# All 32 cache pages of the samples issued from GpSimd's queue, in order, each as its buffer comes free

## The reference, cut to what matters

```python
k_p, v_p = shared_kv(hp, kv_norm, w_kv, pos_p)
k_s, v_s = shared_kv(hs, kv_norm, w_kv, pos_s)
n_seq = page_table.shape[0]                                   # 8 samples
k_past = cache_k[page_table].reshape(n_seq, -1, ATTN_N_HEADS, 2, ATTN_HEAD_DIM)
v_past = cache_v[page_table].reshape(n_seq, -1, ATTN_N_HEADS, ATTN_V_DIM)

def diff_attn_sample(q, k_past, v_past, k_new, v_new, lam):
    s_past = jnp.einsum('bqhjd,bkhjd->bhjqk', q, k_past).astype(jnp.float32) * scale
    s_new = jnp.einsum('bqhjd,bkhjd->bhjqk', q, k_new).astype(jnp.float32) * scale
    ...
    p = jax.nn.softmax(jnp.concatenate([s_past, s_new], axis=-1), axis=-1)
    att = (p[:, :, 0] - lam * p[:, :, 1]).astype(v_new.dtype)
    return (jnp.einsum('bhqk,bkhe->bqhe', att[..., :past], v_past) + jnp.einsum('bhqk,bkhe->bqhe', att[..., past:], v_new))
```

## Time and profile before

| | us |
|---|---|
| runs: median of 3 (lowest, highest) | 1665.21 (1665.15, 1666.52) |
| profiled execution, its own time | 1660.28 |
| its span, first to last instruction | 1658.4 |
| PE busy | 1570.6 (95%) |
| DVE, ACT, POOL busy | 944.6, 717.6, 16.5 |
| mean granted TensorE clock, share of 2.4 GHz | 0.953 |

### The profile page before, as it was taken

How to read it: one execution, slowest core, us unless ns; L and a number is a source line. 1 busy time by engine, 2 the same in 40 slices (tenths; PEclk the granted TensorE clock), 3 DMA queues, 4 the chain that set the end, 5 groups by cost and what they waited for, 6 DMA issues and landing times.

```text
span 1658.4 us, 29697 instructions
## 1 busy us (share of the span) xinstructions
PE 1570.6 (95%) x12252; PEld 1490.1 (90%) x12252; DVE 944.6 (57%) x1577; ACT 717.6 (43%) x1590; POOL 16.5 (1%) x20
## 2 busy tenths in 40 slices
PE   7999789997999999999999999998989999999997
PEld 6999556996899999999998988887878999999997
DVE  5667777799536742245346868852235752344435
ACT  5435445899425541243224436653245542134321
POOL 0000010000000000000000000000000000000000
PEclk8999999998899999999999999997579999999998
DMA  4222100564221322222222134431412322232221
GB/s 147 82 77 90 39 21 14 204 229 178 77 92 62 115 90 80 99 102 90 90 89 78 64 106 150 141 128 65 139 59 69 103 90 90 77 109 96 77 102 52
DMA packets 46088, 160.15 MB, mean 97 GB/s; under 512 B 5122, under 2 KB 7554, under 8 KB 45954
## 3 DMA queue, kind: packets, MB, share of 16 engines
q1 hardware_dynamic: 45954, 158.25, 27.9%
HBM read 142.07 MB, written 16.16 MB: 95 GB/s over the span
## 4 chain that ended last, share of the span: by engine, by line
PE 78%; DVE 11%; ACT 5%; DMA 4%; issue 2%; SPq 0%; DVEq 0%; ACTq 0%
PE GP L514 17%; PE GP L515 17%; PE GP L516 17%; PE WP L514 5%; PE WP L515 5%; PE WP L516 5%; PE WP L897 2%; DMA sssm<-hs 1%; PE GP L848 1%; DMA hs<-ssm_in 1%; DVE wL L1380 1%; PE GP L672 1%; PE WP L870 1%; ACT ht L1121 1%; PE GP L659 1%
## 5 line engine op out<-in xcount | busy, mean ns | idle before, releaser
L514 PE MATMUL GP<-hidH,wH 128*128 128x260 f32 x1408 | 414.5, 294 | 4.6 <-DVE hidL L1561 4.6
L514 PE MATMUL GP<-aH,wH 128*128 128x260 f32 x1376 | 395.9, 288 | 11.3 <-DVE aL L1406 5.8
L515 PE MATMUL GP<-hidL,wH 128*128 128x260 f32 x1408 | 401.9, 285 | 0.0
L516 PE MATMUL GP<-hidH,wL 128*128 128x260 f32 x1408 | 401.1, 285 | 0.0
L515 PE MATMUL GP<-aL,wH 128*128 128x260 f32 x1376 | 392.1, 285 | 0.0
L516 PE MATMUL GP<-aH,wL 128*128 128x260 f32 x1376 | 391.7, 285 | 0.0
L1380 DVE TENSOR_TENSOR wL<-wraw,wH 128x1024 fp32r<-128x1024 f32 x216 | 260.8, 1222 | 100.9 <-ACT wH L1003 100.5
L1003 ACT ACTIVATE wH<-wraw 128x1024 fp32r<-128x1024 f32 x216 | 225.4, 1053 | 153.7 <-DMA wraw<-wblk 152.9
L514 PEld LDWEIGHTS GP<-hidH,wH 128*128 128x128 f32 x1408 | 269.5, 191 | 10.4 <-DVE hidL L1561 5.5
L514 PEld LDWEIGHTS GP<-aH,wH 128*128 128x128 f32 x1376 | 262.6, 191 | 14.4 <-issue 11.1
L515 PEld LDWEIGHTS GP<-hidL,wH 128*128 128x128 f32 x1408 | 269.9, 192 | 1.9 <-issue 1.5
(11 more groups left out here) (268 smaller groups left out, 2228.5 us busy)
## 6 DMA issues: line engine op xcount, KB each, us to landing
wraw<-wblk SPq DMA_DIRECT2D x216, 512.0 KB, 3.4
hs<-ssm_in SPq DMA_DIRECT2D x16, 512.0 KB, 3.6
sssm<-hs SPq DMA_DIRECT2D x16, 512.0 KB, 4.5
ktile<-kcache SPq DMA_DIRECT2D x16, 512.0 KB, 4.0
vtile<-vcache SPq DMA_DIRECT2D x16, 512.0 KB, 5.6
hT<-x_t SPq DMA_DIRECT2D x4, 520.0 KB, 6.5
kt_out<-kT SPq DMA_DIRECT2D x4, 520.0 KB, 6.6
vt_out<-vT SPq DMA_DIRECT2D x4, 520.0 KB, 5.1
```

The source lines that it names most:

```text
L514: pe.matmul(out, lh, rh, start=first, stop=False)
L515: pe.matmul(out, lh, rl, start=False, stop=False)
L516: return pe.matmul(out, ll, rh, start=False, stop=last)
```

## The change

SP's loop loses all page issues, with their `value_load`s and the waits on `ss_s` and `pv_mm`. It keeps weight loads and outputs. GpSimd gets the 32 issues behind its products: first the key pages, page n as soon as page n - 2 has been scored, then, when all 16 pages have been scored, the value pages, page n as soon as the `page_values` that read buffer n % 4 before has ended. The conditions on which a buffer counts as free are those of before. PE, DVE and ACT run the same instructions in the same order.

```diff
@@ -448,35 +448,11 @@
-        sp.wait_ge(pt_in, 16)
-
-        def page(n, cache, dst, i, s):
-            idx = sp.value_load(ptile[0:1, n:n + 1], min_val=0, max_val=cache.shape[0] - 1)
-            sp.dma_start(dst[:, i, :, :].rearrange("p h k -> p (h k)"),
-                         cache[bass.ds(idx, 1), :, :].rearrange("o p n -> p (o n)")).then_inc(s[i], 16)
-
         kvb = BLOCK0["kv"] + RING
         stream(kb, kvb)
-        sp.wait_ge(done, PLACE["kv", 0, 0])
-        for n in range(2):
-            page(n, kcache, ktile, n, kp_in)
         for t in range(37):
             if t % 2 and t < STEPS:
                 load(kvb + t // 2)
-            if t - 1 in SPREAD_AT:
-                for n in range(2 * SPREAD_AT[t - 1] + 2, 2 * SPREAD_AT[t - 1] + 4):
-                    if n < NB * PAGES:
-                        sp.wait_ge(ss_s, n - 1)
-                        page(n, kcache, ktile, n % 2, kp_in)
-            if t == 23:
-                sp.wait_ge(ss_s, NB * PAGES)
-                for n in range(4):
-                    page(n, vcache, vtile, n, vp_in)
-            if PAGES_AT.get(t - 1, NB) + 2 < NB:
-                b = PAGES_AT[t - 1]
-                sp.wait_ge(pv_mm, b + 1)
-                for n in (2 * b + 4, 2 * b + 5):
-                    page(n, vcache, vtile, n % 4, vp_in)
             if t % 8 == 0 and t >= 8:
@@ -506,6 +482,23 @@
+        def page(n, cache, dst, i, s):
+            idx = pool.value_load(ptile[0:1, n:n + 1], min_val=0, max_val=cache.shape[0] - 1)
+            pool.dma_start(dst[:, i, :, :].rearrange("p h k -> p (h k)"),
+                           cache[bass.ds(idx, 1), :, :].rearrange("o p n -> p (o n)")).then_inc(s[i], 16)
+
+        pool.wait_ge(pt_in, 16)
+        pool.wait_ge(done, PLACE["kv", 0, 0])
+        for n in range(NB * PAGES):
+            if n >= 2:
+                pool.wait_ge(ss_s, n - 1)
+            page(n, kcache, ktile, n % 2, kp_in)
+        pool.wait_ge(ss_s, NB * PAGES)
+        for n in range(NB * PAGES):
+            if n >= 4:
+                pool.wait_ge(pv_mm, n // 2 - 1)
+            page(n, vcache, vtile, n % 4, vp_in)
```

## The result

The changed kernel takes 1653.39 us (median of 20 runs; the kernel before beside it 1666.46). The ratio is 0.9926, 95% interval 0.9908 to 0.9945, that is 12.3 us less, with bounds of 9.2 and 15.3. One of the 20 runs of the kernel before took 2533 us; without it their median is 1666.40. Two later comparisons gave 0.9944 (0.9926 to 0.9962) and 0.9942 (0.9919 to 0.9964), 9 to 10 us less. The forecast was 9.8 less and 1655.4. The profiled execution took 1651.82, its span 1650.1.

The account below looks back on a forecast made before the run. TensorE, 95% busy, was taken to lose time to value pages 4 and 5 standing in SP's queue behind a waiting load; -7.4 - 2.8 + 0.4 = -9.8 us, so 1665.2 to 1655.4 us, range 1651 to 1664.5.

Parts of the forecast that it names:

- The wait: TensorE's 7.4 us wait for a value page ahead of the value pass for sequence 2 goes away: -7.4 us.
- The pass of sequence 2: The value pass right behind the stall starts at full clock, taking a mean 4.2 us against 6.96: -2.8, bounds -3.5 and 0.
- What follows the pass: Work behind the value pass for sequence 2 runs at a somewhat lower clock: +0.4 us, bounds 0 and 0.8.
- Value pages 0 to 3: First four value pages, issued some 6 us earlier, first used at 1110.84: 0 us, hidden before and after.
- SP's loads at 0: Weight loads left in SP's queue are still issued when TensorE ends a half tile: 0 us gained.
- Key pages: Key pages issued from POOL stay covered ahead of VectorE's products: 0 us, upper bound +3.6.
- the price of an issue: For POOL's pages, buffer free to landed takes 5 to 6 us, bounds 4.7 and 9.7; a pair's second page some 1 us more.
- the limit: Sign against the price step: a landing time of over 8 us for a page issued by POOL would break it.
- rival 1: Without the stall's rest the clock falls around the value passes and takes back 9.6 us: no change, 1665.0 us; 7%.
- another queue saves only issue time: Rival: moving page issues to POOL wins only the 1.1 us step between two issues: no change, 1664.1 us; 7%.
- POOL did not hold VectorE: Rival judged here: POOL's 16 key page issues each hold VectorE 1.02 us, +6.5 in sum: slower, 1671.7 us; 10%.
- the better outcome: Rival: denser work holds the clock up behind sequence 2 and through sequence 3, 1.8 and 1.2 us more: 1652.4 us; 6%.

## Why the prediction was right, and where it was not

**The cause was right.** The stall was a place in SP's program order. Moving the pair ahead of the load on SP itself gives the gain, and putting the wait back on POOL takes it away.

**The wait, -7.4:** P1 to P2 fell from 18.04 to 10.62, by 7.42. This term carried most of the sum and came out as read.

**The pass of sequence 2, -2.8 (bounds -3.5 and 0):** it fell from 6.96 to 3.47, by 3.49, the bound. The clock was 1.00 throughout (stretch of the changed kernel):

```profile
1135.20:1138.70 3.50, 3.50 (x35) 3.48 (x33) 0.00 (x0) 1.97 (x4) 0.00 (x0) 1.00 0.42 150
```

The term was mis-sized by the choice of a mean over three passes. Two of them, 4.32 and 4.70, were slowed in part (granted clock 0.84 and 0.70), the third, 3.47, was not (1.00). Those two had begun in a stretch at 1.00 just as this pass was forecast to, so the rows did not say which of them it would follow. In the nine executions without the stall it took 3.47 to 3.74.

**What follows the pass, +0.4:** P2 to P3 without the pass was 11.81 and is 11.72, so nothing.

**Value pages 0 to 3, "0, hidden both times":** this step failed. The pages themselves are hidden, but the forecast asked only who waits for the pages, not what they are put ahead of. It had read that POOL would issue them some 6 us earlier, and it put SP's loads at 0, since they "stay gated by PE"; the load's issue is indeed gated, but the gate does not fix when it lands. The landing grew from 3.8 to 7.36 us and cost +1.84 (1.4 and 1.2 in the other two executions).

**Key pages and the price of an issue:** no loss, as forecast. Timeline of DVE (the reduction that frees the buffer of key page 4) and, in a second fence, the list of DMAs (KB each, median us from issue to landing), both of the changed kernel:

```profile
996.24 1.22 DVE L1735 TENSOR_REDUCE sT<-ktile 128x16 f32<-128x1024 f32 x1
```

```profile
wraw<-wblk SPq DMA_DIRECT2D x216, 512.0 KB, 3.4
...
ktile<-kcache POOLq DMA_DIRECT2D x16, 512.0 KB, 3.6
vtile<-vcache POOLq DMA_DIRECT2D x16, 512.0 KB, 4.3
```

From the end of the work that frees a buffer to the issue it took 1.8 us for key page 4 (end at 996.24 + 1.22 = 997.46, issue 999.24) and 1.2 us for value page 4 (1114.23 + 3.71 = 1117.94, issue 1119.15); the landings of the key pages took 3.6 us in the median, those of the value pages 4.3. That is 5.4 and 5.5, where 5 to 6 was taken and 4.7 to 9.7 were the bounds. The estimate of 3.2 us for a landing lies below both medians. Single landings were longer: value page 3, the last of the four early ones, took 8.0, right at the limit that the forecast had named as breaking this step; PE read that page only in P1. The upper bound was not one: it took the 6.9 of `kt_out` for the slowest transfer of this size, but a 512 KB weight block took 9.9 near the start of the trace of before. A second page comes 1.15 us behind the first (1119.15, 1120.30), forecast 1.

**The sum:** -7.42 - 3.58 + 1.84 = -9.2 in these three steps, beside -9.8 (with +1.2 in place of +1.84 it is -9.8). That the forecast came so close is in part luck: two errors, 0.7 too little for the pass (with its aftermath 1.2) and 1.2 to 1.8 too little for the block, point in opposite ways. The first 20 runs gave -12.3, with -9.8 inside their interval; by the traces the change is worth 9 to 10.

**The rivals.** The clock took nothing back between P2 and P3 (15.19 against the 18.77 of before): it fell to 0.63 at 1138.7 to 1142 and was at 0.94 from there to P3. What rival 1 had feared for the pass of sequence 3 came one pass later, in two of three executions: the pass at P4 took 6.96 where it had taken 4.53, and P4 to E was 1.8 and 2.4 longer than before. In the third it took 4.25, and P4 to E was 0.2 shorter. So this rival is not out; whether the missing rest is the reason is not shown. That another queue saves only issue time is out, as P1 to P2 shows. POOL did not hold VectorE: 1220 ns before and after. Of the better outcome, P3 to P4 gave 0.2 to 0.7 us.

## What to carry to other kernels

Where a transfer is late though its buffer is free and the DMA engines are idle, look at what stands ahead of its issue in the same queue: an issue behind a wait for something else is late by that wait. Here reordering the queue was worth as much as another engine's queue, and it keeps the choice of which transfer goes first. When transfers are released earlier, ask what they are then ahead of on the DMA engines: a transfer that nobody waits for can delay one that somebody waits for. And where executions differ by more than the change, measure between two marks around the changed stage.

## What the runs showed of the hardware that was not expected

A 512 KB block lands in 3.4 us in the median, but in 6.55 to 7.64 in the six executions in which POOL's four pages of the same size were issued up to 4.6 us ahead of it. From 1088 to 1098 us of the changed kernel, while these pages and the block were under way, the DMA engines were 0.90 busy and moved 301 GB/s:

```profile
1088.00:1098.00 10.00, 10.00 (x78) 8.30 (x77) 3.93 (x9) 4.24 (x14) 1.06 (x2) 1.00 0.90 301
```

The first of POOL's DMAs after a long rest showed 0.72 us, the others 0.53 to 0.54, and back to back they mostly stood 1.15 us apart, about SP's own step: four pages from SP took 4.01 with 0.34 for one record, (4.01 - 0.34) / 3 = 1.2.
